# 100 early U chunks instead of 64, and other owners of the low weight parts beside G

## The reference, cut to what matters

```
q      = rms_norm(h) @ w_query             # 8 heads, two halves of 128
a, b   = top 16 keys of 128 for each half; the best 16 sums of the 256 pairs
expert = 128 * a + b ; gate = softmax(score)          # 8 * 16 experts a token
out    = sum over a token's experts of gate * gelu(h . u[expert]) * v[expert]
```

## Time and profile before

| what | value |
|---|---|
| median of 3 runs | 1556.12 us (1554.26 to 1560.02) |
| span of the profiled execution | 1548.2 us |
| TensorE busy | 1435.7 us, 93% |
| VectorE, ScalarE, GpSimd busy | 1175.8, 684.5, 674.5 us |
| first product for G, first early V block, start of the late chunks | 403.08, 592.30, 788.54 us |

### The profile page before, as it was taken

The page is one execution under the profiler, slowest core; times in us unless marked ns, Lnnn a source line. Parts: engine busy times, 40 slices in busy tenths (PEclk is TensorE's granted clock), DMA queues, the critical chain, the costliest instruction groups (busy, mean ns, idle before and its releaser), DMA issues.

```text
span 1548.2 us, 31404 instructions
## 1 busy us (share of the span) xinstructions
PE 1435.7 (93%) x11038; PEld 1350.0 (87%) x11038; DVE 1175.8 (76%) x2036; ACT 684.5 (44%) x1035; POOL 674.5 (44%) x300
## 2 busy tenths in 40 slices
PE   7999898998688889899999999999999989899997
PEld 5776588998688889899999999999999968699997
DVE  4424637889899998888878888888875654499997
ACT  4434544444344443333334444444446346555553
POOL 2313246779444443433434444444433335255441
PEclk9999989999799999999999999999999999999999
DMA  7411045666333335666656655565563323255552
GB/s 277 130 55 41 28 139 188 186 196 178 119 116 113 108 114 169 214 213 213 218 169 188 188 179 181 184 189 183 184 211 119 127 96 112 79 183 184 189 176 81
DMA packets 79624, 240.69 MB, mean 155 GB/s; under 512 B 8896, under 2 KB 25552, under 8 KB 78928
## 3 DMA queue, kind: packets, MB, share of 16 engines
q1 hardware_dynamic: 75744, 228.75, 46.2%
q10 hardware_dynamic: 3824, 11.17, 2.0%
HBM read 229.37 MB, written 10.52 MB: 155 GB/s over the span
## 4 chain that ended last, share of the span: by engine, by line
PE 68%; DVE 25%; issue 3%; ACT 1%; DVEq 1%; DMA 0%; POOL 0%; ACTq 0%
PE ps L1642 36%; PE ps L2019 20%; DVE work L1364 6%; DVE work L1383 3%; DVE work L1365 2%; DVE h_op L1390 2%; DVE w_lo L1042 2%; PE ps L1906 2%; PE ps L1860 1%; DVE h_op L1392 1%; PE ps L1657 1%; DVE big L1351 1%; PE ps L1831 1%; DVE big L1349 1%; PE ps L1880 1%
## 5 line engine op out<-in xcount | busy, mean ns | idle before, releaser
L487 POOL TENSOR_TENSOR w_lo<-raw,w_hi 128x1024 fp32r<-128x1024 f32 x241 | 622.0, 2583 | 748.6 <-ACT w_hi L588 748.6
L1642 PE MATMUL ps<-x_op,w_hi 128*128 128x256 f32 (+1 forms) x3968 | 746.7, 289 | 21.1 <-DVE x_op L1060 8.8
L1642 PEld LDWEIGHTS ps<-x_op,w_hi 128*128 128x128 f32 x3968 | 627.8, 194 | 34.3 <-issue 21.2
L1642 PE MATMUL ps<-x_op,w_lo 128*128 128x256 f32 (+1 forms) x1984 | 567.5, 286 | 0.0
L588 ACT ACTIVATE w_hi<-raw 128x1024 fp32r<-128x1024 f32 x400 | 420.5, 1055 | 270.0 <-PE ps L2019 218.2
L2019 PE MATMUL ps<-h_op,w_hi 128*128 128x256 f32 x2400 | 429.3, 280 | 17.1 <-DVE h_op L1392 14.7
L1642 PEld LDWEIGHTS ps<-x_op,w_lo 128*128 128x128 f32 x1984 | 385.7, 194 | 0.0
L2019 PEld LDWEIGHTS ps<-h_op,w_hi 128*128 128x128 f32 x2400 | 367.0, 188 | 19.8 <-DVE h_op L1392 13.6
L2019 PE MATMUL ps<-h_op,w_lo 128*128 128x256 f32 x1200 | 336.2, 280 | 0.0
L1042 DVE TENSOR_TENSOR w_lo<-raw,w_hi 128x1024 fp32r<-128x1024 f32 x159 | 203.7, 1281 | 39.5 <-ACT w_hi L588 39.3
L2019 PEld LDWEIGHTS ps<-h_op,w_lo 128*128 128x128 f32 x1200 | 225.3, 188 | 0.0
(11 more groups left out here) (267 smaller groups left out, 1079.4 us busy)
## 6 DMA issues: line engine op xcount, KB each, us to landing
raw<-blocks SPq DMA_DIRECT2D x404, 512.0 KB, 3.4
early_store<-kv_mem SPq DMA_DIRECT2D x60, 128.0 KB, 3.2
work<-early_store SPq DMA_DIRECT2D x60, 128.0 KB, 3.3
big<-consts ACTq DMA_DIRECT2D x2, 1336.0 KB, 6.7
big<-h_t ACTq DMA_DIRECT2D x4, 272.0 KB, 3.9
big<-bias_lines ACTq DMA_DIRECT2D x8, 136.0 KB, 2.6
bias_lines<-route_t ACTq DMA_DIRECT2D x4, 264.0 KB, 3.0
res<-mem_t SPq DMA_DIRECT2D x1, 1024.0 KB, 9.2
```

The lines of the kernel that those rows point to most:

```text
L487: pool.tensor_tensor(w_lo[:, s, :], raw[:, s, :], w_hi[:, s, :].bitcast(F32), ALU.subtract).then_inc(sem("lo_pool"), 1)
L1642: mm = pe.matmul(ps[:, m_bank, 0:T], w, x, start=(k == 0 and j == 0), stop=(k == last and j == 2))
```

## The change

100 U chunks are early instead of 64. 20 of them stand alone before G (16 before) and 64 beside it (32), one group of four tokens to a chunk instead of two. From the first block beside G to the second block of the late chunks all low weight parts are VectorE's; GpSimd has none of them. In the early V stage ScalarE, not VectorE, rounds the activations (`act_high`), ahead of the rounding of a weight block in its order. 28 chunks are late instead of 64. SP's loops follow. `layout` is written in terms of EARLY and RING and puts the blocks in the new order.

```diff
--- before.py
+++ after.py
@@ -50,9 +50,9 @@
 LINE = FAR + NQ + 1
 
 PH, NKEYS, TOPK = 8, 128, 16
-EARLY = 64
+EARLY = 100
 SOFT_AT = 5
-EARLY_G = 32
+EARLY_G = NQ // 4
 
 MH, GH, GDK, GDV, CHUNK = 8, 4, 32, 64, 64
 NCH = NQ // CHUNK
@@ -107,7 +107,9 @@
 
     if B_MEM <= n < B_OUT:
         return None
-    return "pool" if B_QUERY <= n <= B_V or n % 2 == 0 else "dve"
+    if B_QUERY <= n < B_PEER + 2:
+        return "pool" if n < B_BESIDE else "dve"
+    return "pool" if n % 2 == 0 else "dve"
 
 
 class At:
@@ -438,10 +440,13 @@
                 if w >= 0 and early(w) is not None:
                     store(At(early(w)), At(M_QUERY + w + 1))
 
-            with sp.Fori(0, (EARLY - 2 * PH) // RING - 2) as i:
+            for k in range(B_BESIDE - B_EARLY):
+                next_load(At(B_EARLY + LOADS_AHEAD + k))
+                store(At(2 * PH + k), At(M_QUERY + 4 * PH + k + 1))
+            with sp.Fori(0, EARLY_G // RING - 2) as i:
                 for j in range(RING):
-                    next_load(At(B_EARLY + LOADS_AHEAD + j, i, RING))
-                    store(At(2 * PH + j, i, RING), At(M_QUERY + 4 * PH + j + 1, i, RING))
+                    next_load(At(B_BESIDE + LOADS_AHEAD + j, i, RING))
+                    store(At(EARLY - EARLY_G + j, i, RING), At(M_PEER - EARLY_G + j + 1, i, RING))
             for j in range(RING):
                 next_load(At(B_V - 2 * RING + LOADS_AHEAD + j))
                 store(At(EARLY - 2 * RING + j), At(M_PEER - 2 * RING + j + 1))
@@ -470,7 +475,9 @@
 
                     sp.wait_ge(sem("act_used"), At(RING + j + 1, i, RING).value())
                     early_back(At(2 * RING + j, i, RING))
-            begin = B_PEER + LOADS_AHEAD - RING
+            begin = B_PEER + LOADS_AHEAD
+            for n in range(begin - RING, begin):
+                next_load(At(n))
             left = N_BLOCKS - begin
             with sp.Fori(0, left // RING) as i:
                 for j in range(RING):
@@ -554,9 +561,10 @@
             los(pool_at[0], B_QUERY + 2)
             norm_lo(R_PEER, NQ)
             los(B_QUERY + 2, B_QUERY + RING)
-            with pool.Fori(1, (B_V - B_QUERY) // RING) as i:
+            with pool.Fori(1, (B_BESIDE - B_QUERY) // RING) as i:
                 for j in range(RING):
                     lo(At(B_QUERY + j, i, RING))
+
             def even(first, end):
 
                 first += first % 2
@@ -566,8 +574,7 @@
                         lo(At(first + j, i, RING))
                 los(first + RING * rounds, end)
 
-            lo(At(B_V))
-            even(B_V + 1, B_IN2 + 2)
+            even(B_PEER + 2, B_IN2 + 2)
             even(B_IN2 + 2, B_OUT2 + 2)
             normalise(U_MOBA, U_X)
             pool_at[0] = B_OUT2 + 2
@@ -863,10 +870,9 @@
 
             def beside(i):
                 for j in range(RING):
-                    for g in range(2 * j, 2 * j + 2):
-                        act.wait_ge(sem("g_product"), At(g + 1, i, 8).value())
-                        act.activation(big[:, bass.ds(At(512 * g, i, 4096).value(), 512)], ps[:, 2 + g % 2, :],
-                                       ACT.Copy).then_inc(sem("g_ready"), 1)
+                    act.wait_ge(sem("g_product"), At(j + 1, i, RING).value())
+                    act.activation(big[:, bass.ds(At(512 * j, i, 512 * RING).value(), 512)], ps[:, 2 + j % 2, :],
+                                   ACT.Copy).then_inc(sem("g_ready"), 1)
                     hi(At(B_BESIDE + 3 + j, i, RING))
                     early(At(EARLY - EARLY_G + j, i, RING), At(M_PEER - EARLY_G + j, i, RING))
 
@@ -875,9 +881,22 @@
             with act.Fori(1, EARLY_G // RING) as i:
                 beside(i)
 
-            with act.Fori(0, EARLY // RING) as i:
+            def act_high(c):
+
+                act.wait_ge(sem("act_used"), c.plus(1).value())
+                if c.first >= 2:
+                    act.wait_ge(sem("block_used"), c.plus(B_V - 1).value())
+                act.activation(h_op[:, c.mod(2), 0, :], hf[:, c.mod(2), :], ACT.Copy).then_inc(sem("act_hi"), 1)
+
+            for c in range(RING):
+                act_high(At(c))
+                if c:
+                    hi(At(B_V + 2 + c))
+            with act.Fori(0, EARLY // RING - 1) as i:
                 for j in range(RING):
-                    hi(At(B_V + 3 + j, i, RING))
+                    act_high(At(RING + j, i, RING))
+                    hi(At(B_V + 2 + RING + j, i, RING))
+            hi(At(B_PEER + 2))
             ahead[0] = B_PEER + 3
 
 
@@ -1358,6 +1377,7 @@
             dve.tensor_tensor(soft_hk, soft_hk, soft_s.rearrange("p a b -> p (a b)").unsqueeze(2).to_broadcast(
                 [P, 2 * PH, TOPK]), ALU.mult).then_inc(sem("route_ready"), 1)
 
+            los(B_BESIDE + 2)
             dve.wait_ge(sem("route_t_ready"), 3)
 
             def one_hot(g, j, tok):
@@ -1365,29 +1385,29 @@
                 return dve.tensor_scalar(one2[:, g, j, :], con("iota"), route_t[:, 1, tok], route_t[:, 2, tok],
                                          ALU.is_equal, ALU.mult)
 
-            for g in range(2):
-                for j in range(4):
-                    ins = one_hot(g, j, slice(4 * g + j, 4 * g + j + 1))
-                ins.then_inc(sem("one_hot_ready"), 1)
-            with dve.Fori(1, NQ // 8) as i:
-                for g in range(2):
-
-                    dve.wait_ge(sem("g_product"), 2 * i + (g - 1))
+            def groups(i, begun=True):
+
+                for g in range(RING):
+                    if begun or g >= 2:
+                        dve.wait_ge(sem("g_product"), At(g - 1, i, RING).value())
                     for j in range(4):
-                        ins = one_hot(g, j, bass.ds(8 * i + (4 * g + j), 1))
+                        ins = one_hot(g % 2, j, bass.ds(At(4 * g + j, i, 4 * RING).value(), 1))
                     ins.then_inc(sem("one_hot_ready"), 1)
-
-
-            def split(c, a, chunk):
+                    lo(At(B_BESIDE + 2 + g, i, RING))
+
+            groups(0, False)
+            with dve.Fori(1, EARLY_G // RING) as i:
+                groups(i)
+
+
+            def weighted(c, a, chunk):
+
+                dve.tensor_tensor(hf[:, c.mod(2), :], a, G[:, :, bass.ds(chunk.value(), 1)].rearrange("p t e -> p (t e)"),
+                                  ALU.mult).then_inc(sem("act_used"), 1)
+
+            def act_low(c):
+
                 b = c.mod(2)
-                dve.tensor_tensor(hf[:, b, :], a, G[:, :, bass.ds(chunk.value(), 1)].rearrange("p t e -> p (t e)"),
-                                  ALU.mult).then_inc(sem("act_used"), 1)
-                dve.wait_ge(sem("act_used"), c.plus(1).value())
-                if c.first >= 2:
-
-                    n = B_V + c.first - 1 if c.first < EARLY + 2 else B_PEER + 2 * (c.first - EARLY) - 1
-                    dve.wait_ge(sem("block_used"), c.value(n, c.stride if c.first < EARLY else 2 * c.stride))
-                dve.tensor_copy(h_op[:, b, 0, :], hf[:, b, :]).then_inc(sem("act_hi"), 1)
                 dve.wait_ge(sem("act_hi"), c.plus(1).value())
                 dve.tensor_tensor(h_op[:, b, 1, :], hf[:, b, :], h_op[:, b, 0, :].bitcast(F32), ALU.subtract
                                   ).then_inc(sem("acts_ready"), 1)
@@ -1395,19 +1415,24 @@
             def early(c):
                 if c.first < RING:
 
-                    split(c, a_out[:, c.mod(RING), :], c.plus(EARLY - RING))
+                    weighted(c, a_out[:, c.mod(RING), :], c.plus(EARLY - RING))
                 else:
                     dve.wait_ge(sem(f"early_loaded{c.mod(RING)}"), c.div(RING) * 16)
-                    split(c, a_in[:, c.mod(RING), :], c.plus(-RING))
-                n = At(B_V + 2 + c.first, c.i, c.stride)
-                if lo_owner(n.first) == "dve":
-                    lo(n)
+                    weighted(c, a_in[:, c.mod(RING), :], c.plus(-RING))
+                act_low(c)
+                lo(At(B_V + 2 + c.first, c.i, c.stride))
 
             def chunk(d):
+                c, b = d.plus(EARLY), d.mod(2)
                 dve.wait_ge(sem("gelu_done"), d.plus(1).value())
-                split(d.plus(EARLY), ge[:, d.mod(2), :], d.plus(EARLY))
-
-            los(B_V + 2)
+                weighted(c, ge[:, b, :], c)
+                dve.wait_ge(sem("act_used"), c.plus(1).value())
+
+                n = B_V + c.first - 1 if c.first < EARLY + 2 else B_PEER + 2 * (c.first - EARLY) - 1
+                dve.wait_ge(sem("block_used"), c.value(n, 2 * c.stride))
+                dve.tensor_copy(h_op[:, b, 0, :], hf[:, b, :]).then_inc(sem("act_hi"), 1)
+                act_low(c)
+
             dve.wait_ge(sem("g_ready"), NQ // 4)
             for c in range(RING):
 
@@ -1994,14 +2019,13 @@
             def beside(i, first=False):
 
                 for j in range(RING):
-                    for g in range(2 * j, 2 * j + 2):
-                        pe.wait_ge(sem("one_hot_ready"), At(g + 1, i, 8).value())
-                        if not first or g >= 2:
```

(12 more changed lines are left out.)

## The result

The changed kernel takes 1540.86 us (median, 1533.09 to 1542.42) beside 1557.05 us for the kernel before: a ratio of 0.9885 (95% interval 0.9853 to 0.9917), 1.1% faster. The forecast was 1535.5 us and 1.3%. In a second set of runs the changed kernel had 1539.78 us beside 1555.5, ratio 0.9891 (0.9865 to 0.9916).

The account below looks back on a forecast made before the run. TensorE was to set the pace beside G, a ScalarE-VectorE loop in early V: 407.0 + 239.4 + 1.5 + 325.6 = 973.5, plus 554.1 gives 1527.6, plus 7.9 gives 1535.5 us; range 1521 to 1556.

Parts of the forecast that it names:

- Start of G: Before the first product for G: four more chunks ahead of the routing wait delay it only 3.9 us, to about 407.0.
- Beside G: Stage building G beside U chunks: TensorE sets the pace, 64 steps of 3.74 us, 239.4 us in all.
- Early V: Early V blocks: 3.26 us a turn, TensorE waiting about 0.43 us in each, 325.6 us, first block 1.5 us late.
- Late: Late stage: 36 U and V pairs of 5.71 us leave it, 205.6 us less.
- The ring: Early V stage: closed path act_high, high part, low part, product, next act_high; 3.26 us a turn against 2.83 of matmuls.
- the first rival: Early V stage runs at TensorE's pace, 2.83 us a block: 42.6 us less, 1493 us; chance 5%.
- the third rival: Early V stage: both ScalarE-VectorE passages cost 0.26 us, a turn 3.65 us, +39 us, 1574 us; chance 6%.
- The second rival: G stage: VectorE still sets the pace, one-hots staying slow; 258.3 us instead of 239.4, 1554 us, no change; chance 8%.
- the reserve: G stage: the skill's caveat that VectorE and GpSimd share a read port, so handing work to GpSimd might not help.
- the fourth rival: V stage: the added pauses of 0.43 us make the clock fall, far slower; chance 1%.
- The offset: Last step, from span to median: 7.9 us between them was kept, turning 1527.6 us into 1535.5.
- the bounds: Whole kernel: the forecast's own limits, 14 us below and 18 above 1535.5, said hardly to fall on one side together.

Follow-up runs that it names:

- x3_gpsimd_low_beside_G: Against the changed kernel, GpSimd again makes the low weight parts beside G and for the first two V blocks; 1552.89 us, ratio 0.9977 to the kernel before.
- x2_vector_rounds: Against the changed kernel, VectorE again rounds the early V activations, and ScalarE's block roundings run one block further ahead; 1491.64 us, ratio 0.959 to the kernel before.
- x6_64_early_port_free: x2_vector_rounds with the earlier chunk counts, 64 early and 32 beside G, VectorE keeping the low parts; 1501.5 us, ratio 0.9655 to the kernel before.
- x0_as_changed: The changed kernel profiled again with no edit; 1533.1 to 1544.0 us in six runs.

## Why the prediction was right, and where it was off

**The stages.** Counted from the query projection, the changed kernel's late stage begins at 739.3 us and the forecast put it at 737.3 (973.5 - 236.2). Start of G: four chunks for 4.4 us (171.2 against 166.8), 3.9 forecast. Beside G: 242.2 with the late first V block, 240.9 forecast; a step is 3.76 us against 3.74. Early V: 325.9 against 325.6. Late: 36 pairs, 207.1 us less, 205.6 forecast. In the PEER layer -19.9 us against -20.6. The first product for G came 171.2 us after the start of the query projection, 170.8 forecast.

**The ring.** Its links measure 0.73, 0.33, 1.07 and 1.15 us (sum 3.28) for 0.71, 0.33, 1.09 and 1.13 (3.26). That it is the cause of the V turn is shown from both sides: opening it takes 43.1 us away (42.6 forecast for the first rival, had it been true), lengthening it by 0.33 us adds 32.3. The hop into act_high, which the third rival would have had at 0.26 us, is 803.96 - 803.23 - 0.62 = 0.11; the hop into the low part is 802.08 - 801.01 - 1.04 = 0.03.

**VectorE beside G.** The second rival is excluded: no one-hot is stretched once GpSimd is silent, and TensorE sets the step with all 64 low parts on VectorE. The advice of the Trainium skill that the prediction weighs (Perfetto Trace Analysis, Optimizing Scalar/DVE Operations) would hand work of a saturated VectorE to GpSimd. Handing the low parts back (x3_gpsimd_low_beside_G) lengthens the stage by 13.5 us, which bears out the reserve that stands beside the advice there.

**The clock in the V stage**, the fourth rival, stayed at 1.00, in spite of a pause in each block.

**The offset.** The step that failed is the last one, from span to median. The prediction kept the 7.9 us between the profiled span and the median as if they belonged to the kernel. Only 1.8 us do: the profiled execution of the changed kernel has a span of 1540.6 and a time of 1542.42. The other 6 us were the profiled execution of the kernel before being a quick one: 1548.2 + 1.8 = 1550.0, where later runs of that kernel go from 1550.19 to 1564.26. The span forecast for the changed kernel, 1527.6, was therefore too low by 13.0 us, of which 12.1 are the stretches ahead (5.7) and behind (6.4). The forecast took both stretches from the quick execution; the changed kernel's had a lower granted clock in them (rows in the last section). The two errors cancel in part, which is luck: 5.4 us are left in the median. The medians fell by 16.2 us where the layer fell by 19.9; the interval, 13 to 23 us, holds both.

**The range.** The upper end of the bounds, +18, was drawn in from a plain sum of 28.5 because bounds hardly fall on one side together. The lower end, -14, is their plain sum all the same. The result needs neither.

**What the change left on the table.** By the prediction's own terms it is a sum of -49 up to the early V stage and +28.7 in it; measured the same way, with the late first V block counted in the V stage, it is -47.4 and +29.0, and -1.5 in the late stage. Moving the low parts off GpSimd pays; moving the rounding of the activations to ScalarE, in this order, takes back 43 us. Of the 64 us between the kernel before and x2_vector_rounds in the PEER layer, 53 come from the owner of the low parts alone (x6_64_early_port_free), 11 from the other chunk counts, and of these about 7 from filling the wait for the routing.

## What to carry to other kernels

When two engines hand work back and forth, write down one turn in the order of each queue and look for a closed path within the same index; its length is a bound that no engine's busy share shows. The remedy is to let one of the two work one index further ahead, if a buffer slot is free for it; here it was, and no work was added. Before relieving a busy engine, ask whether its instructions are long or only held up: here the gain was to give the engine that set the pace more work, and its neighbour none.

## What the runs showed of the hardware

A VectorE instruction that runs beside a GpSimd `tensor_tensor` of 2.4 to 2.5 us (a low weight part) can last until that ends. Beside G it is a `tensor_scalar` of 0.28 or 0.34 us: 32 of 512 take 2.4 to 2.5 us in the kernel before, for 32 low parts, and 64 of 512 take 1.7 to 2.5 us in x3_gpsimd_low_beside_G, for 64. Each ends 0.08 to 0.09 us after a low part. In the changed kernel, with GpSimd silent there, not one of 512 is over 0.35 us. It is not special to that instruction: in the late stage of the changed kernel, where GpSimd works again, the `tensor_tensor` that makes the low activations (L1412) takes 2.3 us in the mean, against 0.43 in the early V stage. TensorE is full there (153.68 of 154 us), so it costs nothing. What VectorE and GpSimd contend for, no run here shows.

TensorE's granted clock over the same instructions behind the PEER layer was between 0.95 (192.4 us, x3_gpsimd_low_beside_G) and 0.91 (199.6 us, x0_as_changed) in the profiled executions. It also moved the stretch ahead. The same 164 matmuls there, in the kernel before and then in the changed one:

```profile
100.68:128.32 27.64, 27.64 (x164) 23.63 (x164) 9.92 (x10) 5.46 (x10) 8.42 (x2) 0.88 0.19 58
```

```profile
101.73:134.03 32.30, 32.30 (x164) 28.12 (x164) 9.92 (x10) 5.46 (x10) 8.41 (x2) 0.74 0.15 49
```

These are 4.7 of the 5.7 us by which the stretch ahead was longer; the other 1.1 stand before the first weight block is multiplied (17.49 against 16.44 us). What decides between the clocks was not tried. A gain of this size is best read within the stages that hold the edit, and the whole from several runs.
